# One 8 KB row per expert in place of two 4 KB rows, in two of three expert gathers

## The chip, the cores and the metric

The kernel runs on one core of one Trainium2 chip. The metric is the time of one execution on the device in microseconds, the median of repeated runs. All arithmetic is float32. The engines are called PE (TensorE), DVE (VectorE), ACT (ScalarE), POOL (GpSimd) and SP (SyncE); the core has 16 DMA engines.

## The reference, cut to what matters

A block of two layers, and then a second block of one layer, work on 256 tokens of width 1024 (the first layer has 256 context tokens too). Each layer ends in a retrieval over 16384 experts: for each token 8 heads pick 16 experts each, so 128 slots a token, with a gate value for each. An expert is a down row and an up row of 1024 numbers.

```python
def _peer(h, w_pq, peer_keys, peer_down, peer_up):
    ...                                       # eidx, gate: (token, 128)
    def one(args):                            # hh: 128 tokens
        hh, ee, gg = args
        a = jnp.einsum("tkd,td->tk", peer_down[ee], hh)
        act = (gg * jax.nn.gelu(a)).astype(hh.dtype)
        return jnp.einsum("tk,tkd->td", act, peer_up[ee])
...
x = x + gate2 * _peer(h2, ...)                # the second block: peer_u, peer_v, exact gelu
```

## The kernel before, in words

Every engine runs its own hand-written program (class `Walk` and its five children); they meet only through semaphores. Tokens lie on the 128 partitions, so a *tile* is 128 tokens, and one *slot* k of a tile is 128 experts, one for each partition. There are three gathers, each over tiles of 128 slots: the first over four tiles (both x and both context tiles of the first layer, 512 slots), the second over two tiles (the second layer, 256 slots), the third over two tiles (the second block, 256 slots).

What `gather` does for slot s of all slots, on each engine:

- POOL issues one indirect DMA that brings 128 down rows of 4 KB to a buffer of `ds` (`fetch`, L3075), and, 18 slots later in the order (`LAG`), one that brings the 128 up rows of that slot to a buffer of `us`. There are `ND = 5` down buffers and `NU = 5` up buffers. A down buffer is free when DVE's dot is done (semaphore `down`); an up buffer when PE has used it (`up_tensor`), and DVE too in odd tiles (`up_vector`).
- DVE makes the dot: one SCALAR_TENSOR_TENSOR (L906, 128x1024) of the down row with the token's row, which lies in PSUM (`HP`), with a sum into `AA[:, k]`.
- ACT makes the gelu of 16 dots at once (`GK = 16`), DVE multiplies the 16 by the gates (`weighted`), and ACT makes for each slot a 128x128 diagonal matrix of its weights (`dg`, four of them, L2462).
- PE adds weight times up row: it multiplies the diagonal matrix with the up row into PSUM, columns 0 to 511 (`ap`) and in even tiles columns 512 to 1023 (`av`). In odd tiles DVE does the second half with a 128x512 SCALAR_TENSOR_TENSOR. A 128x512 product in float32 shows as two MATMULs.
- After 128 slots `fold` multiplies both sums by the gate row and adds them to x.

The reason for the lag of 18 slots is the order of these steps: an up row can be used only when its group of 16 weights is made.

Beside a gather, `weave` runs other work in each engine's program, some units between two slots at a rate: queries, top-k of the later heads (on which POOL waits by `routed` before slots 0, 32 and 64), and in the second gather the norm and the first projections of the second block. During the first half of the second and third gathers there is such work; later there is little of it in the third.

POOL also issues the loads of the modulation weights (`modhalf`, L3021) ahead of the gathers. DMAs issued by POOL use descriptor space whose size is `dynamic_dma_scratch_size`, 8192 bytes a partition.

Of the kernel before, what the change touches and what calls it, by code (L numbers as in the profile page):

```python
# [81 lines left out]
BRANCH = (("w_oa", 4), ("w_ob", 2), ("w_oc", 2))  # L82
ND = NU = 5
GK = 16
LAG = GK + 2
NEXT = 128

# [46 lines left out]
class Walk:  # L134
# [3 lines left out]
    def __init__(self, e, K):  # L138
        self.e, self.K, self.S = e, K, K.S
        self.got, self.put, self.known, self.latest, self.before = {}, {}, {}, None, None  # L140
        self.uses = [0] * 8
        self.rings = {k: Ring(v) for k, v in RINGS.items()}
        self.ring = self.rings["wide"]
        self.slots = {k: Ring(v) for k, v in SLOTS.items()}
        self.slot = self.slots["three"]
        self.wuse, self.wfull = [0] * 5, [0] * 5
        self.rows, self.units = 0, 0
        self.base, self.shared, self.gathers = 0, 0, 0
        self.halves_in = 0
        self.zs = {}  # L150
        self.outs, self.turned_in, self.closed_in, self.wq = {}, {}, {}, {}
# [335 lines left out]
    def gather(self, tiles, tables, gelu, rows):  # L487
        total = NEXT * len(tiles)
        for s in range(total + LAG):
            yield (tiles[s // NEXT], s % NEXT // 32) if s < total and s % 32 == 0 else None  # L490
        self.base += total
        self.shared += total // 2

    def down_place(self, s):
# [87 lines left out]
    def main(self):  # L582
# [171 lines left out]
        def queries_then_second(queries):  # L754
# [7 lines left out]
            self.second_asked()  # L762
            yield ("after", NEXT + LAG - 4)
            self.second_vectors()
            yield ("after", NEXT + LAG + 2)
            self.folded(5)
# [3 lines left out]

        self.weave(self.gather([0, 1], tables, gelu, [(1, 0, 5), (1, 0, 5)]), queries_then_second(queries), RATE1, done=done)
        self.folded(6)
# [64 lines left out]
        self.weave(self.gather([0, 1], (A["peer_u_2"], A["peer_v_2"]), gelu2, [(2, 0, 5), (2, 0, 5)]),  # L837
                   last_queries(queries), RATE2, done=done)
# [47 lines left out]
class Vector(Walk):  # L886
# [414 lines left out]
    def peer_pick(self, l, t, m, ha, hb, meanwhile=None):  # L1301
# [26 lines left out]
        self.stt(e0, e0, 128.0, ES[:, 1, hs, :], M, AD)  # L1328
        if l == 1:
            self.ts(e0, e0, 16384.0, None, AD, None)  # L1330
        ks = slice(16 * ha, 16 * hb)
# [16 lines left out]
    def gather(self, tiles, tables, gelu, rows):  # L1348
# [46 lines left out]
        self.gathers += 1  # L1395

    def fold(self, t, c, n0, gr, g_in):

        K, S = self.K, self.S
        self.wait_ge(*g_in)  # L1400
        self.wait_ge(S.up_tensor, c + 1)
        self.tt(K.tpb, K.ap, gr[:, 0:512], M)
        self.tt(self.X(t)[:, 0:512], self.X(t)[:, 0:512], K.tpb, AD)
        self.tt(K.tpb, K.av, gr[:, 512:1024], M, inc=self.inc(S.sum_read))
        self.tt(self.X(t)[:, 512:1024], self.X(t)[:, 512:1024], K.tpb, AD, inc=self.inc(S.tile_done))
        self.mark(("row", n0))
# [289 lines left out]
class Tensor(Walk):  # L1696
# [438 lines left out]
    def gather(self, tiles, tables, gelu, rows):  # L2135
# [20 lines left out]
        self.gathers += 1  # L2156

    def keys_there(self):
        self.wait_ge(*self.next(self.S.keys_in, 16))
# [297 lines left out]
class Scalar(Walk):  # L2457
# [327 lines left out]
    def gather(self, tiles, tables, gelu, rows):  # L2785
# [3 lines left out]
        for s in range(total + LAG):  # L2789
# [27 lines left out]
        self.base += total  # L2817

    def folded(self, n):
# [183 lines left out]
class Pool(Walk):  # L3003
# [26 lines left out]
    def gather(self, tiles, tables, gelu, rows):  # L3030
# [34 lines left out]
        self.gathers += 1  # L3065

    def freed(self, n, total):
# [163 lines left out]
def memory(nc, ctx, K):  # L3231
    K.NB = NB = 53200
    K.arena = arena = ctx.enter_context(nc.sbuf_tensor("arena", [128, NB + 2 * D], F32))
# [24 lines left out]
    K.GR = GR = here()  # L3258
    K.BG, K.GR2 = GR + 9728, GR + 4096
# [4 lines left out]
    K.ds, K.us = [gm(D) for _ in range(ND - 1)] + [more(D)], [gm(D) for _ in range(NU - 1)] + [more(D)]  # L3264
    K.dg, K.AA, K.AW = [gm(128) for _ in range(4)], [gm(128) for _ in range(2)], [gm(128) for _ in range(2)]
    K.tpb = gm(512)
    K.HP, K.ap, K.av = K.psum[:, 0:1024], K.psum[:, 1024:1536], K.psum[:, 1536:2048]
# [72 lines left out]
def semaphores(nc, ctx):  # L3340
# [14 lines left out]
    S.row_in_psum, S.down, S.activated, S.weighted = one("row_in_psum"), one("down"), one("activated"), one("weighted")  # L3355
    S.down_in, S.up_in = several("down_in", ND), several("up_in", NU)
    S.diagonal, S.up_vector, S.up_tensor = one("diagonal"), one("up_vector"), one("up_tensor")
# [55 lines left out]
def layout(inputs):  # L3413

    f = {k: np.ascontiguousarray(inputs[k]) for k in _NAMES}
    f["peer_down"] = np.asarray(inputs["peer_down"]).reshape(2 * 16384, D)
    f["peer_up"] = np.asarray(inputs["peer_up"]).reshape(2 * 16384, D)
    f["peer_u_2"] = np.asarray(inputs["peer_u_2"]).reshape(16384, D)
    f["peer_v_2"] = np.asarray(inputs["peer_v_2"]).reshape(16384, D)
    vecs = [np.asarray(inputs[k]).reshape(128, 8) for k in ("c", "c_ctx", "c_2")]  # L3420
# [33 lines left out]
```

## Time and profile before

| | us |
|---|---|
| time before, median of 3 (lowest, highest) | 4169.66 (4167.23, 4174.44) |
| span of the profiled execution | 4362.9 |
| first and last issue of the first gather | 446.8, 2063.4 |
| first and last issue of the second gather | 2269.4, 3060.9 |
| first and last issue of the third gather | 3605.4, 4348.8 |

The page gives only the span for the profiled execution; it is 193.2 us (4.6%) longer than the median of the unprofiled runs. Times inside the profile are on that longer scale. The page shows busy shares of the engines over the whole span, the same in 40 slices of 109 us, the DMA queues, the costliest groups of instructions and the chain of work that ended last. In the names of the profile `in_peer_down` and `in_peer_up` are the tables of the first two gathers, `in_peer_u` and `in_peer_v` those of the third, and `arena` is all of SBUF.

### The profile page before, as it was taken

To read this page: it belongs to the slowest core of one execution; us is meant where nothing else is said; L and a number is where in the kernel's file an instruction comes from. 1 tells how busy PE (TensorE), PEld (TensorE's weight loads), DVE (VectorE), ACT (ScalarE), POOL (GpSimd) and SP (SyncE) were. 2 spreads that over 40 slices of the span, in tenths; PEclk is the share of its full clock that TensorE was granted. 3 is DMA by queue.
4 is the path that set the end of the run, shared out by engine and by line. 5 is a ranking of instruction groups with operands and counts; after the bars stand their busy time and mean duration, and the time that the engine had idled before them with its cause. 6 is when DMAs were issued, how large, how long until landed. Compare 5 with 4: busy or idle time off the path is not lost.

```text
span 4362.9 us, 35889 instructions
## 1 busy us (share of the span) xinstructions
PE 3358.4 (77%) x11238; PEld 1715.0 (39%) x11238; DVE 2577.2 (59%) x5454; ACT 816.5 (19%) x1926; POOL 2040.9 (47%) x2148
## 2 busy tenths in 40 slices
PE   6889686888767787887687766766878887866766
PEld 2357442356434243551354422221366654422111
DVE  1412768566686846676357674666563347684776
ACT  1311111321211122121211111111231211111111
POOL 0210566655555666666116665566000005676665
PEclk9999899999979899996899988866988998999556
DMA  6663998999999999999849999999400039999999
GB/s 228 227 237 130 338 363 320 375 356 409 401 362 355 343 378 352 392 410 375 298 159 369 333 365 392 372 405 374 157 1 1 1 113 338 352 350 372 379 369 346
DMA packets 380787, 1330.31 MB, mean 305 GB/s; under 512 B 39500, under 2 KB 44876, under 8 KB 377016
## 3 DMA queue, kind: packets, MB, share of 16 engines
q0 software_dynamic: 313344, 1141.10, 69.3%
q1 hardware_dynamic: 61104, 164.18, 10.1%
q10 hardware_dynamic: 6152, 22.74, 1.4%
q8 instruction: 93, 1.52, 0.1%
q14 instruction: 94, 0.77, 0.1%
HBM read 1326.69 MB, written 1.17 MB: 304 GB/s over the span
## 4 chain that ended last, share of the span: by engine, by line
PE 15%; DVE 10%; DMA 9%; issue 7%; POOL 5%; another core or an unknown queue 3%; ACT 2%; ACTq 0%; DVEq 0%; POOLq 0%
PE ps L1701 15%; POOL arena L3075 5%; DMA arena<-in_peer_up,arena 5%; DVE arena L893 3%; DVE arena L906 3%; DMA arena<-in_peer_v,arena 2%; ACT arena L2462 1%; DMA arena<-in_ada_w 1%; DMA arena<-in_peer_u,arena 1%; DMA arena<-in_peer_down,arena 1%; PE ps L1707 1%; DVE arena L914 1%; DVE arena L1287 1%; DVE arena L1282 0%
## 5 line engine op out<-in xcount | busy, mean ns | idle before, releaser
L1701 PE MATMUL ps<-arena 128*128 128x512 f32 (+9 forms) x10500 | 3254.6, 490 | 873.9 <-ACT arena L2462 231.9
L1701 PEld LDWEIGHTS ps<-arena 128*128 128x128 f32 (+4 forms) x10500 | 1621.6, 196 | 2435.2 <-issue 1844.2
L906 DVE SCALAR_TENSOR_TENSOR arena<-arena,ps 128x1024 f32<-128x1024 f32 x1024 | 1240.6, 1217 | 542.1 <-DMA arena<-in_peer_down,arena 289.1
L3075 POOL DMA_INDIRECT arena<-in_peer_down,arena x768 | 747.1, 973 | 654.8 <-DVE arena L910 269.5
L3075 POOL DMA_INDIRECT arena<-in_peer_up,arena x768 | 736.5, 959 | 541.2 <-PE ps L1701 294.3
L2462 ACT ACTIVATE arena<-arena 128x128 f32<-128x128 f32 (+5 forms) x1242 | 444.4, 387 | 1890.8 <-PE ps L1701 636.3
L3075 POOL DMA_INDIRECT arena<-in_peer_u,arena x256 | 248.4, 970 | 647.9 <-DVE arena L910 543.6
L906 DVE SCALAR_TENSOR_TENSOR ps<-arena,ps 128x512 f32<-128x512 f32 x508 | 383.4, 755 | 143.0 <-DMA arena<-in_peer_up,arena 88.8
L2462 ACT ACTIVATE arena<-ps 128x512 f32<-128x512 f32 (+4 forms) x349 | 191.5, 549 | 1165.6 <-PE ps L1701 547.9
L3075 POOL DMA_INDIRECT arena<-in_peer_v,arena x256 | 242.4, 947 | 149.2 <-issue 59.9
L893 DVE TENSOR_TENSOR arena<-arena 128x512 f32<-128x512 f32 (+8 forms) x398 | 246.9, 620 | 72.1 <-ACT arena L2462 42.1
L893 DVE TENSOR_TENSOR arena<-ps,arena 128x512 f32<-128x512 f32 (+3 forms) x192 | 131.3, 684 | 254.8 <-PE ps L1701 220.8
L1707 PE MATMUL ps<-arena 128*128 128x128 f32 (+2 forms) x738 | 129.6, 314 | 124.5 <-DVE arena L893 68.5
L893 DVE TENSOR_TENSOR arena<-arena,ps 128x256 f32<-128x256 f32 (+1 forms) x134 | 73.0, 545 | 222.7 <-PE ps L1701 171.2
L1707 PEld LDWEIGHTS ps<-arena 128*128 128x128 f32 (+2 forms) x738 | 97.8, 157 | 205.8 <-issue 108.6
L2462 ACT ACTIVATE arena<-ps,arena 128x256 f32<-128x256 f32 (+2 forms) x140 | 71.2, 508 | 423.1 <-PE ps L1701 260.4
L910 DVE COPY arena<-ps 128x512 f32<-128x512 f32 (+5 forms) x69 | 39.6, 574 | 172.2 <-PE ps L1701 124.0
L2462 ACT ACT_TABLE_LOAD x81 | 103.9, 1283 | 56.1 <-DVE arena L893 29.8
L1277 DVE MAX8 arena<-ps 128x8 f32<-128x128 f32 x128 | 28.6, 288 | 137.9 <-PE ps L1701 98.7
L3021 POOL DMA_DIRECT2D arena<-in_w_mod x40 | 30.6, 765 | 132.0 <-PE ps L1701 69.6
L906 DVE DVE_READ_ACCUMULATOR arena<-arena,ps 128x1 f32 x1024 | 86.3, 84 | 0.0
L914 DVE TENSOR_REDUCE arena<-ps 128x1 f32<-128x512 f32 (+2 forms) x50 | 30.3, 607 | 81.9 <-PE ps L1701 69.4
(34 smaller groups left out, 565.1 us busy)
## 6 DMA issues: line engine op xcount, KB each, us to landing
arena<-in_w_mod POOLq DMA_DIRECT2D x40, 1024.0 KB, 6.6
arena<-in_gate_blocks SPq DMA_DIRECT2D x16, 2048.0 KB, 7.8
arena<-in_w_in SPq DMA_DIRECT2D x14, 2048.0 KB, 7.9
arena<-in_w_pq SPq DMA_DIRECT2D x13, 2048.0 KB, 16.0
arena<-in_ada_w POOLq DMA_DIRECT2D x24, 1024.0 KB, 8.3
arena<-in_w_out SPq DMA_DIRECT2D x8, 2048.0 KB, 8.0
arena<-in_gate_blocks SPq DMA_DIRECT2D x8, 1792.0 KB
arena<-mod_scratch ACTq DMA_DIRECT2D x26, 512.0 KB
```

The costliest lines, as they stand in the source:

```text
L893: self.e.tensor_tensor(o, a, b, op).then_inc(*(inc or self.inc(self.S.vec)))
L906: self.e.scalar_tensor_tensor(o, a, s, b, op0, op1, accum_out=accum).then_inc(*(inc or self.inc(self.S.vec)))
L910: self.e.tensor_copy(o, a).then_inc(*(inc or self.inc(self.S.vec)))
L914: self.e.tensor_reduce(o, a, AX, op).then_inc(*(inc or self.inc(self.S.vec)))
L1277: e.max(v[j][:, 0:8], src[j]).then_inc(*self.inc(S.vec))
L1287: e.match_replace(tmp[j], v[j][:, 0:8], src[j], NEG).then_inc(*self.inc(S.vec))
L1701: return self.e.matmul(o, l, r, start=start, stop=stop)
L1707: ins = self.e.transpose(o, x, self.K.ident)
L2462: self.e.activation(o, i, f, bias=bias, scale=scale, accum_out=accum).then_inc(*(inc or self.inc(self.S.act)))
L3021: self.e.dma_start(K.sums[place].rearrange("p (k n) -> p k n", n=512), rows[:, 4 * half:4 * half + 4, :]).then_inc(S.sums_in[place], 16)
L3075: self.e.indirect_dma_start(out=o, out_offset=None, in_=table, in_offset=bass.IndirectOffsetOnAxis(ap=idx.bitcast(U32), axis=0)).then_inc( ...
```

## The change

The second and third gathers use a new `gather_pairs`. The host lays the down row and the up row of an expert side by side, so that one indirect DMA of POOL brings both to one buffer (`pairs`): 8 KB a partition. The second gather has six such buffers, the third nine. The lag is one slot (`NEAR = 1`): ACT makes the weight of each slot by itself, right after its dot, with three instructions (gelu of 128x1, multiply by the gate, diagonal matrix), and PE and DVE add the up row one slot behind the dot. DVE no longer multiplies groups of 16. A buffer is free when PE has used its up half (and DVE in odd tiles), so the down half stays held with it.

The first gather keeps its form, with six down and six up buffers (`ND = NU = 6`). `fold` writes its product into the gate row in place of a buffer of its own. The expert numbers of the second layer are no longer shifted by 16384. The arena grows by 1536 words and the descriptor space shrinks from 8192 to 2048 bytes a partition. The hold points of `weave` in the second gather stay where they were, written as numbers.

```diff
-ND = NU = 5
+ND = NU = 6
+NEAR = 1
@@ Vector @@
+    def gather_pairs(self, tiles, table, gelu, rows):
+        base, total, ones = self.base, NEXT * len(tiles), self.base - 4 * NEXT
+        for s in range(total + NEAR):
...
+                d, there = self.pair_place(s)
+                self.wait_ge(*there)
+                self.stt(d[:, 0:D], d[:, 0:D], 1.0, K.HP, M, M, inc=self.inc(S.down), free=True, accum=K.AA[n % 2][:, k:k + 1])
+            u = s - NEAR
...
+                if n % 2:
+                    src, w = self.pair_place(u)[0][:, 1536:2048], K.AW[n % 2][:, k:k + 1]
+                    self.wait_ge(S.weight_one, ones + u + 1)
...
+                        self.stt(K.av, src, w, K.av, M, AD, inc=self.inc(S.up_vector), free=True)
@@ Tensor @@
+                buf, there = self.pair_place(u)
+                self.wait_ge(*there)
+                self.wait_ge(S.diagonal, c + 1)
...
+                ins = self.mm(K.ap, K.dg[c % 4], buf[:, 1024:1536], k == 0, k == NEXT - 1)
+                if n % 2 == 0:
+                    ins = self.mm(K.av, K.dg[c % 4], buf[:, 1536:2048], k == 0, k == NEXT - 1)
+                ins.then_inc(*self.inc(S.up_tensor))
@@ Scalar @@
+                w = K.AW[n % 2][:, k:k + 1]
+                self.wait_ge(S.down, c + 1)
+                self.act(w, K.AA[n % 2][:, k:k + 1], gelu, inc=self.inc(S.gelu_one), free=True)
+                self.wait_ge(*self.own())
+                self.act(w, w, ACT.Copy, scale=K.GT[:, tiles[n], k:k + 1], inc=self.inc(S.weight_one), free=True)
+                self.wait_ge(*self.own())
+                self.wait_ge(S.up_tensor, c - 3)
+                self.act(K.dg[c % 4], K.ident, ACT.Copy, scale=w, inc=self.inc(S.diagonal), free=True)
@@ Pool @@
+                self.freed(max(0, s - len(K.pairs[self.gathers]) + 1), total)
+                o, there = self.pair_place(s)
+                self.fetch(o, table, K.EI[:, tiles[n], k:k + 1], there[0])
@@ memory @@
-    K.NB = NB = 53200
+    K.NB = NB = 54736
+    common = [gm(2 * D) for _ in range(ND - 1)] + [more(2 * D)]
+    K.pairs = {1: common, 2: common + [arena[:, NB - 2 * D * i:NB - 2 * D * (i - 1)] for i in (3, 2, 1)]}
@@ layout, kernel @@
+    f["peer_rows"] = np.concatenate([down[1], up[1]], 1)
-    nc = bacc.Bacc("TRN2", target_bir_lowering=False, num_devices=1, dynamic_dma_scratch_size=8192)
+    nc = bacc.Bacc("TRN2", target_bir_lowering=False, num_devices=1, dynamic_dma_scratch_size=2048)
```

## Rows read from the trace of the kernel before

**Rows 1.** The page, parts 1 and 2: busy time, DMA in 40 slices.

```profile
PE 3358.4 (77%) x11238; PEld 1715.0 (39%) x11238; DVE 2577.2 (59%) x5454; ACT 816.5 (19%) x1926; POOL 2040.9 (47%) x2148
...
DMA  6663998999999999999849999999400039999999
GB/s 228 227 237 130 338 363 320 375 356 409 401 362 355 343 378 352 392 410 375 298 159 369 333 365 392 372 405 374 157 1 1 1 113 338 352 350 372 379 369 346
```

**Rows 2.** Windows by stage: busy us (instructions) of each engine, clock, DMA share, GB/s.

```profile
core 0: us, PE busy (x) PEld busy (x) DVE busy (x) ACT busy (x) POOL busy (x), PEclk, DMA share, GB/s
...
446.00:2072.00 1626.00, 1279.23 (x3733) 665.67 (x3733) 1095.32 (x2392) 322.17 (x810) 988.85 (x1024) 0.89 0.97 370
...
2269.00:3066.00 797.00, 569.49 (x1327) 232.67 (x1328) 514.65 (x1068) 122.95 (x312) 494.68 (x512) 0.81 0.97 372
...
3603.00:3880.00 277.00, 209.91 (x768) 115.44 (x768) 196.93 (x568) 43.14 (x105) 176.65 (x184) 0.93 0.95 351
3880.00:4000.00 120.00, 86.07 (x163) 31.42 (x164) 70.73 (x118) 20.71 (x51) 82.01 (x82) 0.91 0.96 359
4000.00:4340.00 340.00, 232.99 (x261) 59.51 (x260) 233.78 (x362) 49.29 (x130) 226.48 (x241) 0.59 0.99 372
```

**Rows 3.** Windows inside the last tile of the third gather.

```profile
4030.00:4055.00 25.00, 17.87 (x19) 4.74 (x20) 19.73 (x30) 3.22 (x8) 18.80 (x20) 0.57 1.03 410
4062.00:4100.00 38.00, 25.47 (x26) 6.31 (x26) 25.85 (x41) 5.93 (x15) 25.34 (x27) 0.54 0.97 351
```

**Rows 4.** Groups by form, 4000 to 4300: busy us, mean ns, idle before.

```profile
L1701 PE MATMUL ps<-arena 128*128 128x512 f32 x228 | 206.8, 1011 | 92.7 <-DMA arena<-in_peer_v,arena 57.6 <-issue 29.9 <-ACT arena L2462 2.8
L906 DVE SCALAR_TENSOR_TENSOR arena<-arena,ps 128x1024 f32<-128x1024 f32 x107 | 130.7, 1221 | 71.9 <-DMA arena<-in_peer_u,arena 48.9 <-issue 22.9
L3075 POOL DMA_INDIRECT arena<-in_peer_v,arena x107 | 100.5, 939 | 68.5 <-PE ps L1701 29.1 <-issue 23.0 <-remote 16.1
...
L906 DVE SCALAR_TENSOR_TENSOR ps<-arena,ps 128x512 f32<-128x512 f32 x98 | 74.0, 755 | 18.0 <-DMA arena<-in_peer_v,arena 9.7 <-issue 4.3
...
L2462 ACT ACTIVATE arena<-arena 128x128 f32<-128x128 f32 x105 | 41.6, 402 | 239.3 <-PE ps L1701 109.8 <-issue 69.6 <-remote 54.1
L906 DVE DVE_READ_ACCUMULATOR arena<-arena,ps 128x1 f32 x107 | 8.9, 83 | 0.0
L2462 ACT ACTIVATE arena<-arena 128x16 f32<-128x16 f32 x7 | 1.5, 217 | 17.9 <-issue 17.6
```

**Rows 5.** Timeline of the DMA issues on GpSimd, 4049 to 4073.

```profile
4053.85 0.94 POOL L3075 DMA_INDIRECT arena<-in_peer_u,arena  x1 [0.30 <-issue]
4057.07 0.94 POOL L3075 DMA_INDIRECT arena<-in_peer_v,arena  x1 [2.28 <-issue]
...
4061.99 0.94 POOL L3075 DMA_INDIRECT arena<-in_peer_v,arena  x1 [2.73 <-PE ps L1701]
...
4064.84 0.94 POOL L3075 DMA_INDIRECT arena<-in_peer_v,arena  x1 [0.66 <-issue]
...
4067.70 0.94 POOL L3075 DMA_INDIRECT arena<-in_peer_v,arena  x1 [0.69 <-issue]
```

**Rows 6.** DMA queues in 4030 to 4055, a stretch of the third gather.

```profile
DMA packets 2814, 10.26 MB, mean 410 GB/s; under 512 B 310, under 2 KB 310, under 8 KB 2814
...
q0 software_dynamic: 2814, 10.26, 102.7%
```

**Rows 7.** DMA queues in 300 to 310, loads of 16 KB a partition.

```profile
DMA packets 95, 1.29 MB, mean 129 GB/s; under 512 B 16, under 2 KB 16, under 8 KB 16
...
q1 hardware_dynamic: 94, 1.28, 29.9%
```

**Rows 8.** Timeline of the end, 4352 to 4363.

```profile
4355.58 0.75 DVE L906 SCALAR_TENSOR_TENSOR ps<-arena,ps 128x512 f32<-128x512 f32 x1 [0.52 <-DMA arena<-in_peer_v,arena]
...
4356.89 0.69 DVE L893 TENSOR_TENSOR arena<-ps,arena 128x512 f32<-128x512 f32 x1 [0.55 <-PE ps L1701]
...
4359.06 0.69 DVE L893 TENSOR_TENSOR arena<-arena 128x512 f32<-128x512 f32 x1
```

More of the change, by code:

```diff
@@ L492, in gather, with pair_place, pairs_done @@
         self.shared += total // 2
+        self.gathers += 1
+    def gather_pairs(self, tiles, table, gelu, rows):
+        total = NEXT * len(tiles)
+        for s in range(total + NEAR):
+            yield (tiles[s // NEXT], s % NEXT // 32) if s < total and s % 32 == 0 else None
+        self.pairs_done(total)
+    def pair_place(self, s):
+        bufs = self.K.pairs[self.gathers]
+        i = s % len(bufs)
+        return bufs[i], (self.S.pair_in[i], 16 * (self.pair_uses[i] + s // len(bufs) + 1))
+    def pairs_done(self, total):
+        n = len(self.K.pairs[self.gathers])
+        for i in range(n):
+            self.pair_uses[i] += len(range(i, total, n))
+        self.base += total
+        self.shared += total // 2
+        self.gathers += 1
     def down_place(self, s):
@@ L769, in queries_then_second @@
                 yield from self.z_block(0, j)
-        self.weave(self.gather([0, 1], tables, gelu, [(1, 0, 5), (1, 0, 5)]), queries_then_second(queries), RATE1, done=done)
+        self.weave(self.gather_pairs([0, 1], A["peer_rows"], gelu, [(1, 0, 5), (1, 0, 5)]), queries_then_second(queries), RATE1, done=done)
         self.folded(6)
@@ L1395, in gather, with gather_pairs @@
         self.gathers += 1
+    def gather_pairs(self, tiles, table, gelu, rows):
+        K, S = self.K, self.S
+        base, total, ones = self.base, NEXT * len(tiles), self.base - 4 * NEXT
+        for s in range(total + NEAR):
+            n, k = divmod(s, NEXT)
+            yield (tiles[n], k // 32) if s < total and k % 32 == 0 else None
+            if s < total:
+                if k == 0:
+                    self.wait_ge(*self.next(S.row_in_psum))
+                d, there = self.pair_place(s)
+                self.wait_ge(*there)
+                self.stt(d[:, 0:D], d[:, 0:D], 1.0, K.HP, M, M, inc=self.inc(S.down), free=True, accum=K.AA[n % 2][:, k:k + 1])
+            u = s - NEAR
+            if u >= 0:
+                n, k = divmod(u, NEXT)
+                c = base + u
+                if n % 2:
+                    src, w = self.pair_place(u)[0][:, 1536:2048], K.AW[n % 2][:, k:k + 1]
+                    self.wait_ge(S.weight_one, ones + u + 1)
+                    if self.halves(u):
+                        self.wait_ge(S.up_vector, self.halves(u))
+                    if k == 0:
+                        self.wait_ge(S.tile_done, c // NEXT)
+                        self.ts(K.av, src, w, None, M, None, inc=self.inc(S.up_vector), free=True)
+                    else:
+                        self.stt(K.av, src, w, K.av, M, AD, inc=self.inc(S.up_vector), free=True)
+                if k == NEXT - GK:
+                    gate = self.row()
+                if k == NEXT - 1:
+                    self.fold(tiles[n], c, *gate)
+        self.pairs_done(total)
     def fold(self, t, c, n0, gr, g_in):
@@ L2817, in gather, with gather_pairs @@
         self.base += total
+        self.gathers += 1
+    def gather_pairs(self, tiles, table, gelu, rows):
+        K, S = self.K, self.S
+        base, total = self.base, NEXT * len(tiles)
+        for s in range(total + NEAR):
+            n, k = divmod(s, NEXT)
+            yield (tiles[n], k // 32) if s < total and k % 32 == 0 else None
+            if s < total:
+                c = base + s
+                if k == 0:
+                    self.wait_ge(S.down, c)
+                    self.act(K.HP[:, 0:512], K.H2[:, tiles[n], 0:512], ACT.Copy)
+                    self.act(K.HP[:, 512:1024], K.H2[:, tiles[n], 512:1024], ACT.Copy, inc=self.inc(S.row_in_psum))
+                w = K.AW[n % 2][:, k:k + 1]
[6 more added lines that the diff above has]
+                self.act(K.dg[c % 4], K.ident, ACT.Copy, scale=w, inc=self.inc(S.diagonal), free=True)
+            u = s - NEAR
+            if u >= 0 and u % NEXT == NEXT - GK:
+                self.take_mod(*rows[u // NEXT])
+        self.pairs_done(total)
     def folded(self, n):
@@ L3065, in gather, with gather_pairs @@
         self.gathers += 1
+    def gather_pairs(self, tiles, table, gelu, rows):
+        K, S = self.K, self.S
+        total = NEXT * len(tiles)
+        for s in range(total + NEAR):
+            n, k = divmod(s, NEXT)
+            yield (tiles[n], k // 32) if s < total and k % 32 == 0 else None
+            if s < total:
+                if k in K.routed_at[tiles[n]]:
+                    self.wait_ge(*self.next(S.routed))
+                self.freed(max(0, s - len(K.pairs[self.gathers]) + 1), total)
+                o, there = self.pair_place(s)
+                self.fetch(o, table, K.EI[:, tiles[n], k:k + 1], there[0])
+        self.pairs_done(total)
     def freed(self, n, total):
@@ L3263, in memory @@
     more = Mem(arena, (NB, NB + 2 * D))
-    K.ds, K.us = [gm(D) for _ in range(ND - 1)] + [more(D)], [gm(D) for _ in range(NU - 1)] + [more(D)]
+    common = [gm(2 * D) for _ in range(ND - 1)] + [more(2 * D)]
+    K.ds, K.us = [p[:, 0:D] for p in common], [p[:, D:2 * D] for p in common]
+    K.pairs = {1: common, 2: common + [arena[:, NB - 2 * D * i:NB - 2 * D * (i - 1)] for i in (3, 2, 1)]}
     K.dg, K.AA, K.AW = [gm(128) for _ in range(4)], [gm(128) for _ in range(2)], [gm(128) for _ in range(2)]
-    K.tpb = gm(512)
     K.HP, K.ap, K.av = K.psum[:, 0:1024], K.psum[:, 1024:1536], K.psum[:, 1536:2048]
```

42 lines of the change are left out of this document (27 added, 15 removed).

## The prediction, made before the change was run

> **What bounds the kernel now.** I read the page first [rows 1]. PE is busy 77% of the span, but the slices say more: in all three gathers the DMA engines are at 9 tenths or more, at 340 to 410 GB/s. The windows by stage say it in numbers [rows 2]: 0.97 of the DMA engines in the first and second gather, 0.95, 0.96 and 0.99 in the three parts of the third. The gathers are transfers first of all; but 0.97 busy came with 372 GB/s in one place and a full engine can do more, so I looked inside one quiet tile [rows 3]. For 25 us the core moved 410 GB/s, and then for 38 us 351 GB/s at a share of 0.97. So there are two things to win: the dips, and the price of each packet.
>
> The dips come from the issue side. A slot is 1 MiB; at 410 GB/s it takes 1.0486/0.410 = 2.56 us. POOL needs two issues for it, and their starts stand 0.94 + 0.30 = 1.24 us apart when it waits for nothing [rows 5], so 2.49 us a slot. It is hardly faster than the engines, and after a loss it can't refill the queue. The issue at 4057.07 came after 2.28 us of idleness and that at 4061.99 after 2.73, charged to PE; from then on the up rows went out every 2.85 us (4061.99, 4064.84, 4067.70), and that is the stretch with 351 GB/s. An average slot in 4000 to 4300 takes 300/107 = 2.80 us [rows 4].
>
> **The change part by part.** The sum is made on the profile's scale, against its span of 4362.9 us; the median is 4169.66, 0.956 of that, and I scale the end result by it.
>
> *Packets of 8 KB.* In the quiet stretch the 4 KB packets number 2814 - 310 = 2504, in 1.027 x 25 x 16 = 411 us of engine time [rows 6]: 164 ns each. Loads of 16 KB a partition [rows 7] show 94 - 16 = 78 packets in 0.299 x 10 x 16 = 47.8 us: 613 ns each. A line through both gives 164 + (613 - 164)/3 = 314 ns for 8 KB, where two of 4 KB cost 328: 4.4% less, 0.11 us a slot. Over the 512 slots of the two gathers 56 us if the engines set the pace all the time. Early in both gathers top-k and queries stand beside them, so I take three quarters: -42 us. Below: 0, if the engines get the 8 KB in two packets all the same; above: -56.
>
> The Trainium skill speaks against this term: DMA: Bandwidth & Descriptors, section "SWDGE vs HWDGE vs iDMA", has a packet at "≤4096 B preferably" for DMAs that GpSimd issues. By that the term would be 0 and not -42. The trace has no indirect row above 4 KB to test it; the rival below carries its chance.
>
> *One issue in place of two.* POOL then needs 1.24 us for what takes the engines 2.4 to 2.6, and refills at once after a wait; the third gather may have nine slots out, the second six, where five downs and five ups were shared before. The room: from 3880 to 4340 the third gather moved 120 x 0.359 + 340 x 0.372 = 169.6 MB in 460 us; at 410 GB/s it is 414, so 46 us of dips. I take two thirds, -30 us; bounds 0 (PE really is the pace, a rival) and -46. In 3603 to 3880 (277 us at 351 GB/s: 40 us of room) and in the second gather (797 at 372: 74 us) DVE is at 71% and 65% and PE at 76% and 71% [rows 2], with work that must be done before later slots are routed; of those 114 us I take -10, between 0 and -50.
>
> *Six buffers in the first gather.* It moves 370 GB/s over 1626 us [rows 2], with 159 us of room, but DVE (67%) and PE (79%) hold it, and a sixth buffer adds one slot to five. I take -8, between 0 and -25.
>
> *The chain of one slot.* Now the weight of a slot is made between its dot and its product. DVE: dot 1.22, its sum 0.08. ACT: gelu of 128x1, not in the trace; the 128x16 one took 0.22 and a narrower one can't be dearer, so 0.22; the multiply by the gate likewise 0.22; the diagonal 0.40 [rows 4]. That makes 0.84 us of ACT a slot, where 0.40 + 0.22/16 was; beside 2.45 us a slot ACT has room (it is busy 14% of the last part). The work is hidden behind the next slot's transfer while PE runs one slot behind. But a pair is now held from landing to product: 1.30 + 0.84 + PE's two products of a slot (2 MATMULs x 1.01 = 2.02 us in the odd tile at a granted clock of 0.59, so mostly at the 1.2 GHz level) = 4.2 us and semaphores, some two slots of the six or nine; four or seven stay in flight, against about eight half slots before. If a background unit holds ACT or DVE in front of it (an evict behind a PE unit, a top-k step), PE waits too, since no 16 finished weights are in store any more. I put +15 on the busy halves of both gathers; bounds 0 and the slower rival.
>
> *Small parts.* DVE loses 32 multiplies of 16 columns, and an add of two in the second layer's top-k: off the path, 0. `fold` has the same four operations, 0.69 each [rows 8]. The drain after the last landing grows: before, the half of 0.75 us stood between landing and fold [rows 8]; now dot, sum, ACT chain and product do, 1.30 + 0.84 + 2.02 - 0.75 = 3.4 us, twice: +7. The first issue of a gather starts as before; the hold points come later than the fold they wait for, 0. The smaller descriptor space also serves `modhalf` and the first gather: 0, with a rival.
>
> Sum: -42 - 30 - 10 - 8 + 15 + 7 = -68 us on 4362.9; times 0.956 it is -65, and 4169.7 - 65 = **4105 us**.
>
> **The rivals.**
>
> *PE is the pace, or the packets stay 4 KB.* For PE: the steady 2.85 us between issues, charged to PE, in a stretch at the 1.2 GHz level. Against: in 4030 to 4055 slots passed at 2.56 us at a granted clock of 0.57. If so the quiet part of the third gather stays, and one of the two large terms goes: -68 + 30 or -68 + 42, times 0.956, so 4133 to 4145 us. Both gone is the next rival.
>
> *It does nothing.* The engines are 97% busy, the bytes are the same, the packets stay 4 KB and every dip comes from the consumers. Then 42 + 30 + 10 go, and +15 + 7 - 8 remain, or less: 4170, within 0.2%.
>
> *The chain is exposed: slower.* Place: the slots with background work, about 96 in each gather. Price: if ACT's 0.84 us stands in the open at each, 192 x 0.84 = 161 us; half of them is 81. With the packets' -42 and no refill gain it gives +39, 4207 us. It outweighs the gains of 82 us (42 + 30 + 10) from about 98 exposed slots on. For: in those stretches PE is 76% busy and waits already for ACT. Against: with one slot of lag, diagonal s is ready while DVE makes dot s+1, unless a unit is longer than a slot.
>
> *The small descriptor space.* If POOL waits for room in it, every gather has that wait, the first too. The trace has no such wait to read, so the price is a small one set against the 0.30 us between two issues: 0.05 us more at each of the first gather's 1024 issues is +51, and with the refill terms lost -42 - 8 + 15 + 7 + 51 = +23, 4192 us. In a sentence of its own, with the Trainium skill's figures (same page, "The descriptor swizzle": nine descriptors an engine for a 128-partition transfer, of 16 B by the page's terms), 2048 B would hold 14 such DMAs, and 12 are the most that the first gather's buffers allow; no run here shows it yet.
>
> *All dips vanish.* -56 - 46 - 50 - 25 + 7 = -170, times 0.956: 4007. I give a case around 4030.
>
> **How the numbers follow.** 0.2% (8 us) is about what a measurement of this kernel can tell from no change. Chances: forecast (4060 to 4132) 0.46; one term missing (4133 to 4145) 0.17; more than forecast (4007 to 4060) 0.07; nothing 0.09; exposed chain 0.16; descriptor space 0.05. Faster is 0.46 + 0.17 + 0.07 = 0.70, same 0.09, slower 0.21. The range 4020 to 4210 leaves out the far end of the best case and about half of the slower ones. The forecast's own range is 4060 to 4132.
>
> **What would show it.** In the new profile: the software queue with under half as many packets for the gathers, some 314 ns each (or as many as before: no packet gain); POOL's busy time some 480 us lower (512 x 0.94), its starts in quiet stretches set by landings; 415 to 430 GB/s there, without stretches near 350; ACT up by some 0.43 us x 512 = 220 us; a slot near 2.5 us in the last tile. Wrong would be: DVE dots waiting for nothing but PE waiting for ACT's diagonals early in the gathers, slots above 3 us there, or a first gather slower than 1626 us.

## The result, and the profile after

The changed kernel took 4148.07 us (median of 4 runs, 4147.20 to 4151.86), the kernel before 4172.05 us in its runs beside it; the ratio is 0.9937, 95% interval 0.9921 to 0.9954. That is 26 us less (19 to 33), where 65 were forecast (4105). The direction is right, and the size is less than half.

The page of the changed kernel, parts 1 and 2, answers to [rows 1]:

```profile
span 4146.8 us, 36783 instructions
PE 3314.7 (80%) x11238; PEld 1698.5 (41%) x11238; DVE 2551.8 (62%) x5418; ACT 1074.4 (26%) x2918; POOL 1544.1 (37%) x1636
...
DMA  6573799999999999999849999899400026999998
GB/s 233 206 263 142 285 400 386 372 380 412 402 403 398 385 372 409 411 410 409 294 145 397 370 393 412 351 411 417 188 21 1 1 87 254 405 394 411 420 420 365
```

The span is about the unprofiled time here. For the kernel before it was 193 us above it, so the two profiles differ by 216 us where the runs differ by 26. Before any comparison of stages the kernel before was therefore profiled once more. The same parts of that second page:

```profile
span 4175.1 us, 35889 instructions
PE 3320.4 (80%) x11238; PEld 1697.3 (41%) x11238; DVE 2579.0 (62%) x5454; ACT 816.2 (20%) x1926; POOL 2035.4 (49%) x2148
...
GB/s 234 208 254 141 307 389 367 377 369 412 403 393 385 381 362 405 409 410 409 300 150 395 391 389 395 362 404 409 190 6 1 1 101 263 387 394 405 409 409 368
```

Slices 37 to 39 of the 40, in the last quiet part, stand at 405, 409 and 409 GB/s. In the first profile they had 372, 379 and 369 [rows 1]. The stretches at 351 GB/s, on which much of the prediction rests [rows 3], belong to that one execution; the second profile has none in this part, and the unprofiled times leave no room for the 193 us. From here on "before" in a comparison of stages is this second profile.

DMA queues in 50 us of the last quiet tile, in the changed kernel (against [rows 6], 410 GB/s in 4 KB packets):

```profile
DMA packets 2881, 20.99 MB, mean 420 GB/s; under 512 B 320, under 2 KB 320, under 8 KB 320
...
q0 software_dynamic: 2879, 20.96, 101.2%
```

Here 2881 - 320 = 2561 packets carry 8 KB, in 1.012 x 50 x 16 = 810 us of engine time: 316 ns each, where 314 were forecast. The packets did become 8 KB. Groups by form in the third gather, 3880 to 4120, answer to [rows 4]:

```profile
L1755 PE MATMUL ps<-arena 128*128 128x512 f32 x190 | 172.5, 1007 | 68.4 <-ACT arena L2538 68.4
L929 DVE SCALAR_TENSOR_TENSOR arena<-arena,ps 128x1024 f32<-128x1024 f32 x95 | 116.0, 1221 | 60.7 <-DMA arena<-in_peer_rows,arena 60.7
L3193 POOL DMA_INDIRECT arena<-in_peer_rows,arena x95 | 89.0, 937 | 152.2 <-PE ps L1755 78.4 <-DVE ps L929 62.0 <-issue 11.8
...
L2538 ACT ACTIVATE arena<-arena 128x1 f32<-128x1 f32 x188 | 46.7, 249 | 151.0 <-DVE arena L929 147.9
```

POOL is idle 152 of 240 us, as expected of one issue a slot (over the whole span it is busy 491 us less than in the second profile of before, ACT 258 more). The two small steps of the chain take 0.25 us each, against an estimate of 0.22. By kind, the gelu takes 0.20 and the multiplication by the gate 0.29. DVE waits for nothing but the transfer. The issues on POOL in the same tile answer to [rows 5]: there is one each 2.5 us, and each follows the release of a buffer.

```profile
3953.68 0.94 POOL L3193 DMA_INDIRECT arena<-in_peer_rows,arena  x1 [1.33 <-DVE ps L929]
3956.17 0.94 POOL L3193 DMA_INDIRECT arena<-in_peer_rows,arena  x1 [1.55 <-PE ps L1755]
3958.68 0.94 POOL L3193 DMA_INDIRECT arena<-in_peer_rows,arena  x1 [1.57 <-PE ps L1755]
```

The end (the timeline's last rows, for [rows 8]) now has the product of the last slot between its dot and the fold:

```profile
4136.36 1.22 DVE L929 SCALAR_TENSOR_TENSOR arena<-arena,ps 128x1024 f32<-128x1024 f32 x1 [0.61 <-DMA arena<-in_peer_rows,arena]
...
4138.73 2.04 PE L1755 MATMUL ps<-arena 128*128 128x512 f32 x2 [0.46 <-ACT arena L2538]
4140.87 0.69 DVE L916 TENSOR_TENSOR arena<-ps,arena 128x512 f32<-128x512 f32 x1 [1.74 <-PE ps L1755]
```

The windows of the three gathers, each from the end of its first dot to the end of its last, answer to [rows 2]:

```profile
457.50:1947.20 1489.70, 1244.97 (x3692) 655.31 (x3691) 1079.28 (x2364) 312.14 (x786) 972.21 (x1010) 0.90 1.01 396
```

```profile
2177.70:2932.20 754.50, 562.46 (x1366) 229.79 (x1366) 499.82 (x1044) 251.28 (x803) 240.55 (x251) 0.83 0.98 391
```

```profile
3475.00:4137.50 662.50, 520.66 (x1246) 203.73 (x1246) 488.16 (x1028) 241.11 (x785) 240.06 (x251) 0.82 1.00 408
```

In the first and third the DMA engines are busy all the time (shares of 1.01 and 1.00); in the second, at 0.98 and 391 GB/s, not quite. Its groups (2177.7 to 2932.2):

```profile
L1755 PE MATMUL ps<-arena 128*128 128x512 f32 (+1 forms) x1350 | 560.5, 560 | 198.5 <-ACT arena L2538 178.5 <-issue 16.9 <-DVE arena L916 2.9
...
L3193 POOL DMA_INDIRECT arena<-in_peer_rows,arena x251 | 241.2, 961 | 503.2 <-PE ps L1755 334.6 <-DVE ps L929 131.1 <-issue 32.7
```

POOL waits 335 us for PE to give a pair back, and PE waits 179 us for ACT's diagonals. The experiments ask which of the two costs time.

A table of the stages, each counted from the end of a gather's first dot in the traces (us). All kernels are told of below:

| kernel | to the first gather | first to second | second to third | third to the end | ratio to before |
|---|---|---|---|---|---|
| before, second profile | 454.0 | 1736.8 | 1293.3 | 691.0 | 1 |
| changed | 457.5 | 1720.2 | 1297.3 | 671.8 | 0.9937 |
| six buffers, no pairs | 455.2 | 1720.8 | 1288.1 | 682.9 | 0.9928 |
| pairs by two issues | 455.9 | 1720.6 | 1310.9 | 684.9 | 0.9996 |
| pairs in the third only | 457.4 | 1719.6 | 1290.9 | 671.1 | 0.9911 |
| changed, lag of three | 459.1 | 1721.4 | 1336.3 | 665.4 | 1.0024 |
| changed, six pairs in the third | 463.1 | 1719.4 | 1294.6 | 687.8 | 0.9963 |
| changed, longer chain | 453.5 | 1720.6 | 1302.6 | 679.9 | 0.9968 |
| third only, lag of three | 457.2 | 1718.3 | 1291.8 | 666.0 | 0.9889 |

The first column should be the same for all and spreads over 10 us; the second, with the first gather in one form in all rows but that of before, over 3. Ratios are each against runs of the kernel before on the same chip; a difference of 0.001 is 4.2 us, and their intervals reach 0.001 to 0.002 to either side.

### The profile page after: what moved, and what is told of

The parts are those of the page before. It is cut to its first block, busy times and chain, and to the rows that moved or that the text cites. A ratio compares the mean times of both kernels' runs of the same rounds, so it can differ in the third digit from the quotient of the medians.

```text
span 4146.8 us, 36783 instructions
## 1 busy us (share of the span) xinstructions
PE 3314.7 (80%) x11238; PEld 1698.5 (41%) x11238; DVE 2551.8 (62%) x5418; ACT 1074.4 (26%) x2918; POOL 1544.1 (37%) x1636
## 4 chain that ended last, share of the span: by engine, by line
PE 19%; DMA 17%; DVE 12%; issue 3%; ACT 2%; POOL 0%; ACTq 0%; DVEq 0%; POOLq 0%
PE ps L1755 18%; DMA arena<-in_peer_rows,arena 15%; DVE arena L916 4%; DVE arena L929 4%; ACT arena L2538 2%; DMA arena<-in_ada_w 1%; PE ps L1761 1%; DVE arena L937 1%; DVE arena L1305 1%; DVE arena L1310 1%; DVE ps L929 1%; DVE arena L1300 0%; DVE arena L1321 0%; DMA arena<-in_peer_up,arena 0%; DVE arena L1315 0%
## 5 line engine op out<-in xcount | busy, mean ns | idle before, releaser
L1755 PE MATMUL ps<-arena 128*128 128x512 f32 (+9 forms) x10500 | 3211.2, 486 | 716.4 <-ACT arena L2538 429.1
L1755 PEld LDWEIGHTS ps<-arena 128*128 128x128 f32 (+4 forms) x10500 | 1604.2, 195 | 2246.8 <-issue 1800.7
L2538 ACT ACTIVATE arena<-arena 128x128 f32<-128x128 f32 (+3 forms) x2234 | 704.1, 326 | 1578.0 <-DVE arena L929 847.0
L3193 POOL DMA_INDIRECT arena<-in_peer_rows,arena x512 | 491.4, 960 | 1532.8 <-PE ps L1755 631.1
L3193 POOL DMA_INDIRECT arena<-in_peer_down,arena x512 | 489.5, 956 | 430.2 <-DVE arena L933 196.8
L3193 POOL DMA_INDIRECT arena<-in_peer_up,arena x512 | 496.6, 970 | 288.2 <-PE ps L1755 166.6
L937 DVE TENSOR_REDUCE arena<-arena 128x32 f32<-128x512 f32 (+7 forms) x64 | 54.6, 854 | 12.3 <-ACT arena L2538 9.8
```

The source lines that it names most:

```text
L937: self.e.tensor_reduce(o, a, AX, op).then_inc(*(inc or self.inc(self.S.vec)))
L1755: return self.e.matmul(o, l, r, start=start, stop=stop)
L2538: self.e.activation(o, i, f, bias=bias, scale=scale, accum_out=accum).then_inc(*(inc or self.inc(self.S.act)))
L3193: self.e.indirect_dma_start(out=o, out_offset=None, in_=table, in_offset=bass.IndirectOffsetOnAxis(ap=idx.bitcast(U32), axis=0)).then_inc( ...
```

## The experiments

**The descriptor space alone.** The kernel before, with

```diff
-dynamic_dma_scratch_size=8192
+dynamic_dma_scratch_size=2048
```

> The kernel before with the descriptor space of the changed one (2048 bytes in place of 8192), nothing else. If the prediction is right that the space costs nothing: within 8 us of the kernel before, 4162 to 4180. The rival of the small descriptor space (0.05 us more at each issue of all gathers, 2048 issues): some 100 us slower in the three gathers, 4270; a tenth of that price would still be +10, 4182.

Measured: 4180.78 us, ratio 1.0008 (0.9998 to 1.0019). It costs nothing that can be measured, 8 us at most, and that rival is gone. The page "DMA: Bandwidth & Descriptors" of the Trainium skill has nine descriptors an engine on each side for a transfer to 128 partitions (section "The descriptor swizzle"), of 16 B each (section "Terms"); by an estimate from these, 2048 / (9 x 16), the smaller space holds 14 DMAs. The runs agree in so far as this one is no slower with up to ten of them out, nor the next with up to twelve.

**Six buffers without pairs.** The kernel before with the memory of the changed one:

```diff
-ND = NU = 5
+ND = NU = 6
-dynamic_dma_scratch_size=8192
+dynamic_dma_scratch_size=2048
```

and `fold` and the arena as changed.

> The kernel before with six down and six up buffers in all three gathers, the small descriptor space and the fold without its own buffer: all of the change but the pairs. The prediction's term for the first gather is -8 (0 to -25), and the same kind of gain in the other two, -4 each: 4155, between 4130 and 4170. The two profiles, read at face value, say more: there the first gather became 101 us shorter (first dot to last dot 1590.8, then 1489.7) in the same form, which would give 4172 - 101 = 4071 or less. If, third, the gain of the profile comes from the profiling itself, which cost the kernel before 193 us and the changed one nothing, this kernel lies at 4160 to 4172 unprofiled, whatever its profile shows.

Measured: 4148.77 us, ratio 0.9928 (0.9915 to 0.9941): 30 us faster, as fast as the whole change (0.9937). The stages say where: 16 us in the first gather, where this kernel and the changed one are the same, then 5 and 8 in the other two. So in the changed kernel the first gather's sixth buffers give 17 us (1736.8 to 1720.2), twice the forecast's 8, and the pairs give 15 us net in the stages of the other two (4 lost, 19 won), where a sixth buffer of each kind gives 13 in the old form.

**Pairs by two issues of 4 KB rows.** The changed kernel, with

```diff
-                self.fetch(o, table, K.EI[:, tiles[n], k:k + 1], there[0])
+                for h in range(2):
+                    self.fetch(o[:, D * h:D * h + D], table[h], K.EI[:, tiles[n], k:k + 1], there[0])
```

> The changed kernel, but each pair is fetched by two issues of 4 KB rows, the down row and the up row, into the two halves of the same buffer; the order, the lag of one slot and the chain on ScalarE stay. Measures packets and issues together. By the prediction's sizes it loses -42 and -40 of the sum, times 0.956: 4148 + 78 = 4226. If the dips are a thing of the profiled execution only, it loses the packets alone, 0.11 us in three quarters of 512 slots: 4148 + 40 = 4188. If neither packets nor issues gave anything unprofiled: 4148, and its packets would still show near 164 ns. Its profile tells whether GpSimd's starts stand 1.24 us apart without waits.

Measured: 4177.19 us, ratio 0.9996 (0.9988 to 1.0005). Against the changed kernel that is 0.0059, 25 us; the stages say 13.6 and 13.1. Packets and issues together are worth 25 to 27 us, not 82. Against the six buffers without pairs, with the same packets and issues, it is 28 us slower: 23 in the second gather, 2 in the third. That is what the form of the pairs costs (the hold, the chain of one slot, the drain); in the third gather it is helped by nine pairs, where the other kernel has six buffers of each kind. The queues in 3950 to 4000 of this kernel:

```profile
DMA packets 5617, 20.46 MB, mean 409 GB/s; under 512 B 624, under 2 KB 624, under 8 KB 5616
...
q0 software_dynamic: 5616, 20.45, 102.6%
```

(5617 - 624) packets in 1.026 x 50 x 16 us are 164 ns each, as before. By packet times two of them cost 329 ns and one of 8 KB 316, 3.9% less. By the rates, 409 against 420 GB/s, a slot is 2.564 and 2.497 us: 0.067 less, not the 0.11 of the prediction.

**Packets or issues.** In the changed kernel GpSimd gets some small fills to do behind each issue, and the packets stay 8 KB:

```diff
+                for _ in range(8):
+                    self.e.memset(K.small[:, 56:60], 0.0).then_inc(*self.inc(S.pad))
+                    self.wait_ge(*self.own())
```

> The changed kernel with 8 small fills of 128x4 on GpSimd behind each issue of a pair, so that GpSimd is busy about as long for a slot as with two issues, while the packets stay 8 KB. Separates the packets from the issues in the 29 us that two issues of 4 KB rows cost. If the packets made the difference (0.069 us a slot in the quiet stretch, 409 against 420 GB/s, and more where the engines refill): 4148 to 4152. If the saved issue did: up to 4148 + 29 = 4177; if half and half, 4162.

Measured: 4240.82 us, ratio 1.0150 (1.0129 to 1.0171), outside both. The timeline of GpSimd in the last tile says why:

```profile
3989.41 0.94 POOL L3196 DMA_INDIRECT arena<-in_peer_rows,arena  x1 [0.65 <-POOL arena L3184]
3990.36 1.24 POOL L3184 MEMSET arena<- 128x4 f32 x8
3992.24 0.95 POOL L3196 DMA_INDIRECT arena<-in_peer_rows,arena  x1 [0.65 <-POOL arena L3184]
```

One slot takes it 0.94 + 1.24 + 0.65 = 2.83 us, more than the engines' 2.50: the pad itself was the pace. So it was run again with five fills and with three.

> The changed kernel with 5 small fills on GpSimd behind each issue of a pair. With eight fills GpSimd needed 0.94 + 1.24 + 0.65 = 2.83 us a slot, more than the 2.50 that the engines take, and became the pace itself. With five it is 0.94 + 5 x 0.155 + 0.65 = 2.37, near the 2.49 of two issues and below the 2.50. If the packets made the 29 us between pairs of one issue and pairs of two: 4148 to 4154. If the saved issue made them: 4170 or more. In between: the share of each.

> The same with 3 fills, 0.94 + 0.465 + 0.65 = 2.06 us a slot. If the time of GpSimd matters through its slack for refilling, the cost grows with the fills: about half of what five cost. If it is packets, 4148 to 4150 here too.

Measured: 4153.76 us, ratio 0.9939 (0.9925 to 0.9952), and 4155.57 us, 0.9943 (0.9929 to 0.9957); the changed kernel has 0.9937. The difference is 1 to 3 us with some 9 to either side, and it doesn't grow with the fills. Within those 9 us, the 25 us are the packets, and the saved issue gave nothing that shows. GpSimd near the pace of the engines (2.38 us a slot with five fills) is no loss as long as it is below it.

**Which of the waits costs.** First the lag: `NEAR = 3`.

> The changed kernel with TensorE and VectorE three slots behind the dot in place of one. Theory A, the chain stands in the open: TensorE waits for ScalarE's diagonals 178 us in the second gather and 138 in the third, and two more slots of lag cover it; 15 to 25 us faster, 4123 to 4133, most of it in the busy halves. Theory B, the buffers are the limit: a pair is held two slots (5 us) longer, and six pairs have no room for it, so the second gather gets slower even in its quiet half (there 6.2 us held plus 5, of 15), by some 0.3 us in 256 slots, 4148 + 80 = 4228, and the third gather with nine pairs stays as it is.

Measured: 4186.33 us, ratio 1.0024 (1.0015 to 1.0033), 36 us slower than the changed kernel. The stages split it: 39 lost in the second gather, 6 won in the third. Theory B holds for six pairs, theory A, and weakly, for nine. Then the number of pairs: the third gather with six.

```diff
-    K.pairs = {1: common, 2: common + [arena[:, NB - 2 * D * i:NB - 2 * D * (i - 1)] for i in (3, 2, 1)]}
+    K.pairs = {1: common, 2: common}
```

> The changed kernel with six pairs in the third gather too, in place of nine. In the changed kernel a pair is held 10 to 17 us in the first tile of the third gather and 6 to 8 us in the second, at 2.5 to 2.7 us a slot. If buffers are the limit beside background work, the first tile comes to look like that of the second gather (3.0 us a slot in place of 2.65): 128 x 0.35 = +45, 4193; the quiet tile stays near 2.53. If six are enough there, 4148.

Measured: 4162.53 us, ratio 0.9963 (0.9949 to 0.9976), 11 us slower; 16 in its stage. The direction is as expected, the size a quarter to a third. The windows of its busy part, here and in the changed kernel (columns as in [rows 2]):

```profile
3477.10:3800.00 322.90, 272.38 (x940) 137.88 (x940) 232.26 (x619) 114.78 (x363) 113.41 (x116) 0.98 0.97 383
```

```profile
3475.00:3800.00 325.00, 283.05 (x968) 143.24 (x968) 238.12 (x633) 120.97 (x387) 121.98 (x125) 0.98 1.00 404
```

The engines have less to do with six (0.97 busy, 383 GB/s) than with nine (1.00, 404), though DVE and PE have room in both.

This run also compares pairs and separate rows at the same buffer memory, six pairs against six buffers of each kind in both gathers: 0.9963 against 0.9928, with intervals that don't touch. Six pairs are 15 us slower, in the stages 6 us in the second gather (1294.6 against 1288.1) and 5 in the third (687.8 against 682.9). So in this kernel pairs gain in the third gather only together with three more buffers. Nine separate buffers of each kind there were not run; how much of the gain the memory alone would bring is not shown.

Last the chain itself, made longer by two multiplications by 1.0:

```diff
+                for _ in range(2):
+                    self.act(w, w, ACT.Copy, scale=1.0, inc=self.inc(S.gelu_one), free=True)
+                    self.wait_ge(*self.own())
```

> The changed kernel with two more 128x1 multiplications by 1.0 on ScalarE in the chain of each slot, in all some 0.6 us more between the dot and the diagonal in 512 slots. Prices the chain. If it stands in the open in the busy halves (about 192 slots, the prediction's slower rival): +0.6 x 192 = +115, 4263, or half of it, 4205. If it is hidden behind the next slot's transfer: under 8 us, 4148 to 4156. Quiet tiles stay at 2.5 us a slot by both.

Measured: 4163.19 us, ratio 0.9968 (0.9956 to 0.9980): 13 us. That is a ninth of the 115 us expected for 192 exposed slots. In quiet tiles the time from dot to diagonal grew by 0.47 us (0.60, then 1.07), so 192 exposed slots would have cost 90 us: a seventh of that was seen. The chain is nearly hidden. What counts for the refill is how long a buffer is held, and the chain is a small part of that.

For the changed kernel the hold was worked out slot by slot. The columns run from the end of the pair's last packet to the start of its dot; from the dot's end to the start of the diagonal; from the diagonal's end to the end of PE's product. With the dot itself (1.22) and the diagonal (0.41) they add up to the time for which the pair is held until PE is done; the last column is the way from the issue to the last packet. Means in us over 32 slots:

```
gather, slots      landed>dot  dot>diagonal  diagonal>product end  held by PE  issue>landed
second, 32 to 63       3.5          1.2              3.7           10.1            6.8
second, 192 to 223     1.9          0.6              2.0            6.2            9.3
third, 32 to 63        8.8          2.5              4.2           17.2            7.9
third, 192 to 223      2.6          0.6              2.0            6.9           14.8
```

The prediction counted 4.2 us. For PE in the quiet slots (192 to 223) that is what dot, chain and product take: 1.22 + 0.6 + 0.41 + 2.0. It left out three things. From the last packet to the last update of the pair's semaphore 1.6 to 2.7 us pass. In the busy slots (32 to 63) a landed pair then waits for DVE, 1.9 us in the second gather and 7.0 in the third, where the quiet slots wait 0.02; and PE's product ends 3.7 and 4.2 us after the diagonal, because other work stands in front. And in the second tiles DVE has its half of the up row only behind the next dot, so the buffer goes back after that: the next issue to it comes 1.3 and 1.0 us after PE's product, in the first tiles 0.3. That is also why the longer chain changes nothing in the quiet tile of the third gather: from semaphore to next issue a pair takes 5.3 us with and without it.

With six pairs in the busy part of the second gather, 10.1 us held, 0.3 to the next issue and 6.8 on the way make the whole cycle of 17.2 us, six slots of 2.87: every buffer is asked for again as soon as it is free. The timeline there shows what makes the holds long:

```profile
2391.84 0.30 PEld L1755 LDWEIGHTS ps<-arena 128*128 128x128 f32 x2 [2.11 <-issue]
2391.87 6.48 PE L1755 MATMUL ps<-arena 128*128 128x512 f32 x20 [1.31 <-ACT arena L2538]
...
2393.73 1.22 DVE L929 SCALAR_TENSOR_TENSOR arena<-arena,ps 128x1024 f32<-128x1024 f32 x1
...
2394.10 0.94 POOL L3193 DMA_INDIRECT arena<-in_peer_rows,arena  x1 [2.34 <-PE ps L1755]
...
2398.59 1.96 PE L1755 MATMUL ps<-arena 128*128 128x512 f32 x4 [0.24 <-ACT arena L2538]
```

PE first waits 1.3 us for a diagonal and then has 20 MATMULs in a row, 12 of three slots and 8 of 128x128 of the top-k's scores; POOL waits 2.3 us for the first of these slots to be done. Both rows of a slot are held up by that. Separate down buffers go back after the dot and don't take part in it.

**Pairs in every gather.** The first gather in pairs too, with six buffers:

```diff
-        self.weave(self.gather([0, 1, 2, 3], tables, gelu, [(0, 0, 5), (0, 0, 5), (0, 1, 5), (0, 1, 5)]),
+        self.weave(self.gather_pairs([0, 1, 2, 3], A["peer_rows_0"], gelu, [(0, 0, 5), (0, 0, 5), (0, 1, 5), (0, 1, 5)]),
```

> The changed kernel with the first gather in pairs too (six pair buffers, 8 KB rows, lag of one slot, weights on ScalarE). If the transfers set its pace, 8 KB packets save 0.11 us in each of 512 slots, 56 us: 4148 - 56 = 4092; if three quarters of them are so paced, 4106. If TensorE and VectorE hold it (84% and 72% busy there) or the chain is exposed beside the background work: 4148 or slower, up to +80 for half of 200 slots at 0.84 us.

Measured: 4237.92 us, ratio 1.0133 (1.0119 to 1.0147), 82 us slower than the changed kernel; the first gather's stage is 1811.6 us, 91 longer. That fits the holds, since this gather has the most background work, but its slots were not taken apart.

**Pairs in the third only.** The second gather in its old form, with six buffers of each kind:

```diff
-        self.weave(self.gather_pairs([0, 1], A["peer_rows"], gelu, [(1, 0, 5), (1, 0, 5)]), ...
+        self.weave(self.gather([0, 1], (A["peer_down_1"], A["peer_up_1"]), gelu, [(1, 0, 5), (1, 0, 5)]), ...
```

> The changed kernel with the second gather back in its old form (separate down and up buffers, six of each, lag of 18 slots); the third stays in pairs. The stages of the profiles say that pairs cost 9 us from the first dot of the second gather to the first dot of the third (1288.1 with six buffers of each kind, 1297.3 changed) and gain 11 us after it (682.9, then 671.8). If the stages add up: 4148 - 9 = 4139, faster than both kernels. If the first stage only handed its delay on or the difference is noise: 4148.

Measured: 4139.74 us, ratio 0.9911 (0.9895 to 0.9926). The stages had put it at 4139. It is faster than the changed kernel by 11 us (0.0026), though the two intervals still overlap a little. With more lag in this kernel, which nine pairs bear, `NEAR = 3` and then `NEAR = 2`:

> Second gather in the old form, third in pairs with TensorE and VectorE three slots behind. By the stages: with three slots of lag the third gather and what follows took 665.4 us in place of 671.8 (first dot to the end), so 4139.7 - 6.4 = 4133; if that difference was between executions only, 4140.

> The same with a lag of two slots. If one more slot is enough to cover the chain: 4133, as with three; if the gain grows with the lag, 4136; if there is none, 4140.

Measured: 4132.82 us, ratio 0.9889 (0.9873 to 0.9906), and 4135.20 us, ratio 0.9894 (0.9878 to 0.9911). The first is 20 us faster than the changed kernel (0.0048), with intervals that don't touch: a version that beats both. Two slots of lag do nearly what three do.

**The kernel before, profiled again.**

> The kernel before, unchanged, profiled once more. Its first profile has a span 193 us above the median of its unprofiled runs, with stretches of 351 GB/s and steady starts every 2.85 us in the last tile; the same kernel with only a smaller descriptor space had a span of 4188.8 and 2.59 us a slot there. If the stretches belonged to that one execution: a span of 4170 to 4190 and 2.59 us a slot in the last tile. If they belong to the larger descriptor space under the profiler: again about 4360 and 2.82.

Measured: span 4175.1 us, 4176.90 us in all, and 2.59 us a slot in the quiet part of the last tile. The first profile's stretches belonged to its execution. A window of the quiet part in this second profile (columns as in [rows 2]), with two issues a slot:

```profile
3880.00:4120.00 240.00, 184.00 (x186) 44.98 (x184) 184.12 (x285) 36.66 (x99) 174.60 (x187) 0.54 1.03 409
```

The engines are full over 240 us, at the rate that the first profile had only in its best stretch (410 GB/s, [rows 3]).

## Why the prediction was wrong in size

The terms, on the scale of the second profile, beside what the runs showed:

| step of the prediction | forecast | measured |
|---|---|---|
| packets of 8 KB | -42 (0 to -56) | -25 |
| one issue in place of two, both parts | -40 (0 to -96) | -1 (some 9 to either side) |
| six buffers in the first gather | -8 (0 to -25) | -17 |
| chain of one slot, and the drain | +22 | +12, net of what more buffers win |
| descriptor space | 0 | 0 |
| sum | -68 | -31 (the unprofiled runs: -26) |

**The step that failed is "One issue in place of two".** It took 46 us of room from the later part of the third gather, at 359 and 372 GB/s with stretches at 351, let POOL's slack win two thirds of it, and added 10 us from the rest: 40 us in all, where 1 was measured, with some 9 to either side. The stretches were real in the one trace, but that execution was 4.6% longer than the median, and in the second profile the quiet part runs at 409 GB/s with two issues a slot: there was no room. Scaling the sum by 0.956 did not help: the excess was not spread evenly. By stages (from one first dot to the next, and to the end) the first profile is 4.9, 3.3 and 8.8% longer than the second, and 9 to 11% a slot in the quiet part, from which most of the term was taken. And POOL at 2.49 us a slot, just below the engines' 2.56, was called hardly faster; the kernels with three and five fills (up to 2.38 beside 2.50) show that just below is enough.

**Packets: right mechanism, size too large.** The packet time of 314 ns was right to 2 ns. With eight packets a slot for each engine the packet times of after still give 8 x (329 - 316) = 0.10 us a slot. But the share is 1.03 with the small packets and 1.01 with the large ones (packet times of one engine overlap a little, and more so the small ones), and by the rates it is 0.067. Of 512 x 0.067 = 34 us 25 came through, the three quarters that were assumed. What the Trainium skill has for a packet, "≤4096 B preferably" (DMA: Bandwidth & Descriptors, section "SWDGE vs HWDGE vs iDMA"), is not borne out here in the way the prediction read it, as a limit to what larger rows win: 8 KB packets moved 420 GB/s and 4 KB ones 409.

**Six buffers: right sign, half the size.** DVE and PE were said to hold the first gather. It gained 17 us from one more buffer of each kind, and the same sixth buffers alone would have given 13 in the others.

**Chain and drain: the size came near by luck, and the cause was another.** Pairs by two issues against the kernel before: +17.6 in the second gather, -6.1 in the third, +12 together, but with six and nine pairs against five buffers of each kind. Against six of each kind it is +23 and +2, so +25. The drain from the last packet to the end grew from 7.8 us (4167.3 to 4175.1) to 10.9 (4135.9 to 4146.8), 3.1 a gather where 3.4 was forecast. The rest is hardly ACT's chain, which took 0.90 us in place of 0.84, but the hold, 6 to 17 us in place of 4.2. That more of it costs in the second gather, and that the third bears it with nine pairs, is what the runs with six and nine pairs and with more lag show.

The time came out just above where the rival "PE is the pace, or the packets stay 4 KB" put it (4133 to 4145). That is luck, for it was for neither of its reasons: the one large term was missing because the dips weren't there to be won. "The chain is exposed" failed: it needed 98 exposed slots to outweigh the gains, and the longer chain cost what some 28 such slots would (13 / 0.47). "It does nothing" was priced wrongly: +15 + 7 - 8 is +14, times 0.956 some 13 us slower, 4183 and not 4170.

## What to carry to other kernels

If a profiled span is some per cent above the unprofiled times, profile again before you price anything by what it shows; a wait or a slow stretch may be that execution's own. Merging two transfers saves their packets' overhead, but the merged buffer is held until its last reader is done: work out the hold from landing to release, with the reader's queue and the lag in it, add the way from issue to landing, and compare the sum with buffers x time per slot. Change one thing in a comparison, and keep the buffer memory equal: here a sixth buffer, a by-product of the change, gave as much as the change, and six pairs lost to six separate buffers of each kind.

## What the runs showed of the hardware that was not expected

- Two profiles of the same kernel: spans of 4362.9 and 4175.1 us, 2.82 to 2.87 and 2.58 to 2.59 us a slot in the quiet part of the same tile, while its unprofiled runs lay within 4167 to 4187. What slowed the first is open.
- Indirect packets of 8 KB: 316 ns, 420 GB/s; of 4 KB: 164 ns, 409 GB/s, both in a quiet tile with the engines full.
- From a pair's last packet to the last update of its semaphore: 1.6 to 2.7 us, in means over 32 slots.
- GpSimd's fill of 128x4 takes 0.10 us, 0.155 with its semaphore, and an indirect DMA behind fills starts 0.65 us after them, where 0.30 lie between two indirect DMAs.
